# A two-layer block with four attention mixers in float32: three engines get written orders of their own

## What is computed

```python
for l in range(DEPTH):
    x = x + 0.5 * swiglu(rms_norm(x, ffn1_norm[l]), ffn1_w_gate[l], ffn1_w_up[l], ffn1_w_down[l])
    p = rms_norm(x, mix_norm[l]) @ w_in[l]            # 2464 columns, split in four
    a = neighbourhood_mixer(...)                      # group A: local attention with a bias
    b = mla_mixer(...)                                # group B: latent q and kv, up-projections
    c = diff_mixer(...)                               # group C: difference of two softmaxes
    d = gqa_mixer(...)                                # group D: grouped heads, rotated q and k
    x = x + concat(a, b, c, d) @ w_out[l]
    x = x + swiglu(...)                               # FFN2; then a norm
```

## Time and profile before

| What | us |
|---|---|
| Median of 3 runs | 1319.37 |
| Lowest and highest of them | 1311.88, 1321.9 |
| The profiled execution | 1319.89 |
| Its span, first to last instruction | 1317.6 |
| First mixer, about | 196 to 346 |
| Second mixer, about | 710 to 862 |

### The profile page before, as it was taken

The page is one execution under the profiler, slowest core; times in us unless marked ns, Lnnn a source line. Parts: engine busy times, 40 slices in busy tenths (PEclk is TensorE's granted clock), DMA queues, the critical chain, the costliest instruction groups (busy, mean ns, idle before and its releaser), DMA issues.

```text
span 1317.6 us, 24755 instructions
## 1 busy us (share of the span) xinstructions
PE 1265.6 (96%) x10500; PEld 1239.5 (94%) x10500; DVE 841.5 (64%) x1059; ACT 640.0 (49%) x850; POOL 78.7 (6%) x57
## 2 busy tenths in 40 slices
PE   6999999988999999999999997999999999999997
PEld 6999999978999999999999996899999989899995
DVE  5766677775676666876667686476666754446665
ACT  4433346754543334533335764453333554766542
POOL 1110011210000000000000211000000000000000
PEclk9999999986999999999999995799999999999999
DMA  8876665320565655566665530256655655415542
GB/s 287 219 227 206 191 224 172 114 87 2 182 200 193 191 191 192 170 199 195 194 219 163 166 132 12 65 165 219 192 191 191 200 178 174 128 58 168 176 152 105
DMA packets 169514, 220.33 MB, mean 167 GB/s; under 512 B 5280, under 2 KB 152480, under 8 KB 169312
## 3 DMA queue, kind: packets, MB, share of 16 engines
q1 hardware_dynamic: 165680, 213.66, 50.8%
q0 software_dynamic: 2080, 2.48, 1.0%
q10 hardware_dynamic: 1680, 3.13, 0.7%
HBM read 218.15 MB, written 3.42 MB: 168 GB/s over the span
## 4 chain that ended last, share of the span: by engine, by line
PE 86%; ACT 6%; DVE 5%; issue 1%; DMA 1%; SPq 0%; POOLq 0%; POOL 0%; DVEq 0%; ACTq 0%
PE pj L433 12%; PE pj L437 12%; PE pj L436 12%; PE acc L437 8%; PE acc L436 8%; PE acc L433 8%; PE tr L433 6%; PE tr L437 6%; PE tr L436 6%; PE acc L616 4%; ACT probs L994 2%; ACT w_hi L875 1%; PE tr L608 1%; DVE w_lo L1186 1%; PE tr L586 1%
## 5 line engine op out<-in xcount | busy, mean ns | idle before, releaser
L1186 DVE TENSOR_TENSOR w_lo<-raw,w_hi 128x2048 fp32r<-128x2048 f32 (+2 forms) x206 | 459.4, 2230 | 241.7 <-ACT w_hi L875 240.3
L875 ACT ACTIVATE w_hi<-raw 128x2048 fp32r<-128x2048 f32 (+2 forms) x206 | 381.2, 1854 | 395.3 <-PE pj L433 142.0
L433 PE MATMUL pj<-hT_hi,w_hi 128*128 128x256 f32 x992 | 277.2, 279 | 3.0 <-DVE w_lo L1186 2.4
L437 PE MATMUL pj<-hT_hi,w_lo 128*128 128x256 f32 x992 | 275.8, 278 | 0.0
L436 PE MATMUL pj<-hT_lo,w_hi 128*128 128x256 f32 x992 | 275.7, 278 | 0.0
L437 PE MATMUL acc<-act_hi,w_lo 128*128 128x256 f32 x704 | 194.3, 276 | 0.0
L433 PE MATMUL acc<-act_hi,w_hi 128*128 128x256 f32 x704 | 194.3, 276 | 0.0
L436 PE MATMUL acc<-act_lo,w_hi 128*128 128x256 f32 x704 | 194.3, 276 | 0.0
L433 PEld LDWEIGHTS pj<-hT_hi,w_hi 128*128 128x128 f32 x992 | 187.5, 189 | 4.5 <-DVE w_lo L1186 2.6
L436 PEld LDWEIGHTS pj<-hT_lo,w_hi 128*128 128x128 f32 x992 | 187.3, 189 | 0.0
L437 PEld LDWEIGHTS pj<-hT_hi,w_lo 128*128 128x128 f32 x992 | 187.1, 189 | 0.0
(11 more groups left out here) (212 smaller groups left out, 1989.6 us busy)
## 6 DMA issues: line engine op xcount, KB each, us to landing
raw<-in_w_in SPq DMA_DIRECT2D x47, 1024.0 KB, 5.3
raw<-in_ffn_w_up SPq DMA_DIRECT2D x44, 1024.0 KB, 5.3
raw<-in_ffn_w_down SPq DMA_DIRECT2D x44, 1024.0 KB, 5.0
raw<-in_ffn_w_gate SPq DMA_DIRECT2D x43, 1024.0 KB, 5.4
raw<-in_w_out SPq DMA_DIRECT2D x12, 1024.0 KB, 4.9
raw<-in_w_proj_a SPq DMA_DIRECT2D x4, 512.0 KB, 3.5
raw<-in_w_proj_b SPq DMA_DIRECT2D x4, 512.0 KB, 3.9
raw<-in_w_proj_c SPq DMA_DIRECT2D x4, 512.0 KB, 3.4
```

What stands on the lines that cost most here:

```text
L433: ins = pe.matmul(out, lhs[0], rhs[0], start=first, stop=False, **kw)
L437: return pe.matmul(out, lhs[1], rhs[0], start=False, stop=last, **kw)
L875: act.activation(w_hi[r % RING][:, 0:w], raw[r % RING][:, 0:w], ACT.Copy).then_inc(hi_set, 1)
L1186: dve.tensor_tensor(w_lo[r % RING][:, 0:w], raw[r % RING][:, 0:w], w_hi[r % RING][:, 0:w].bitcast(F32), ALU.subtract).then_inc(lo_set, 1)
```

## The change

The one list becomes three: ORDER for TensorE (with the norms at its end, since only their numbering is read from it), ORDER_ACT and ORDER_DVE. Looking ahead by two slots is now a step of its own, ("ahead", step), which stands where it is wanted; VectorE's means of x too. In TensorE's list some steps move:

- slots: proj 3 now comes before 4, 6 before 5, 8 before 7 before 9 (it was 9, 7, 8), and wout C before A, B, D;
- latent between scores 0 and 1;
- pv 2 and turn B before probs 3, pv 3 between scores 4 and 5, probs 5 before probs 4, pv 4, score 6, pv 5, score 7 alternating (it was pv 4, probs 5, pv 5, scores 6, 7);
- yturn A before pv 7, yturn C before pv 8 and 9, yturn D between wout C and A.

In ScalarE's list the roundings stand ahead of evacuations, probs 0 before the evacuation of proj 2, and norm D before the copies of probs 3; after the last units yturn C, a rounding, norm yD, yturn B, yturn D. In VectorE's list means comes before the first rounding, prep D still follows scores 4 and 5 and still stands ahead of pv 4, soft 4 and 5 stand together ahead of pv 4, pv 3 ahead of score 4, and scores 8 and 9 ahead of norm yC and yturn A. No instruction's shape or number changes.

```diff
-ORDER = [("proj", 0), ("proj", 1), ("norm", "A"), ("proj", 4), ("prep", "A"), ("proj", 3), ("norm", "latent"),
-         ("turn", "A"), ("prep", "latent"), ("proj", 5), ("score", 0), ("score", 1), ("latent", 0),
-         ("proj", 6), ("norm", "C"), ("soft", 0), ("soft", 1), ("proj", 2), ("probs", 0), ("latent_up", 0),
-         ("prep", "C"), ("probs", 1), ("pv", 0), ("norm", "B"), ("turn", "C"), ("pv", 1), ("score", 2),
-         ("score", 3), ("soft", 2), ("soft", 3), ("proj", 9), ("prep", "B"), ("proj", 7), ("probs", 2),
-         ("norm", "yA"), ("proj", 8), ("probs", 3), ("pv", 2), ("turn", "B"), ("pv", 3), ("norm", "D"),
-         ("score", 4), ("score", 5), ("prep", "D"), ("soft", 4), ("probs", 4), ("pv", 4), ("soft", 5),
-         ("probs", 5), ("pv", 5), ("score", 6), ("score", 7), ("turn", "D"), ("soft", 6), ("soft", 7),
-         ("probs", 6), ("prep", "yA"), ("norm", "yB"), ("probs", 7), ("pv", 6), ("pv", 7), ("norm", "yC"),
-         ("yturn", "A"), ("score", 8), ("score", 9), ("soft", 8), ("prep", "yB"), ("prep", "yC"),
-         ("soft", 9), ("probs", 8), ("probs", 9), ("pv", 8), ("pv", 9), ("yturn", "B"), ("norm", "yD"),
-         ("prep", "yD"), ("yturn", "C"), ("wout", "A"), ("wout", "B"), ("yturn", "D"), ("wout", "C"),
-         ("wout", "D")]
+ORDER = [("proj", 0), ("proj", 1), ("proj", 3), ("proj", 4), ("turn", "A"), ("proj", 6), ("score", 0),
+         ("latent", 0), ("score", 1), ("proj", 5), ("proj", 2), ("probs", 0), ("latent_up", 0), ("probs", 1),
+         ("pv", 0), ("turn", "C"), ("pv", 1), ("score", 2), ("score", 3), ("proj", 8), ("proj", 7), ("probs", 2),
+         ("proj", 9), ("pv", 2), ("turn", "B"), ("probs", 3), ("score", 4), ("pv", 3), ("score", 5), ("probs", 5),
+         ("probs", 4), ("pv", 4), ("score", 6), ("pv", 5), ("score", 7), ("turn", "D"), ("probs", 6), ("probs", 7),
+         ("pv", 6), ("yturn", "A"), ("pv", 7), ("score", 8), ("score", 9), ("probs", 8), ("probs", 9),
+         ("yturn", "C"), ("pv", 8), ("pv", 9), ("yturn", "B"), ("wout", "C"), ("yturn", "D"), ("wout", "A"),
+         ("wout", "B"), ("wout", "D"), ("norm", "A"), ("norm", "latent"), ("norm", "C"), ("norm", "B"),
+         ("norm", "yA"), ("norm", "D"), ("norm", "yB"), ("norm", "yC"), ("norm", "yD")]
+ORDER_ACT = [("ahead", ("proj", 0)), ("ahead", ("proj", 1)), ("proj", 0), ("ahead", ("proj", 3)), ("proj", 1),
+             ("norm", "A"), ("ahead", ("proj", 4)), ("proj", 3), ("proj", 4), ("norm", "latent"), ("turn", "A"),
+             ("ahead", ("proj", 6)), ("proj", 6), ("score", 0), ("score", 1), ("latent", 0), ("ahead", ("proj", 5)),
+             ("proj", 5), ("norm", "C"), ("ahead", ("proj", 2)), ("probs", 0), ("proj", 2),
+             ("ahead", ("latent_up", 0)), ("latent_up", 0), ("probs", 1), ("norm", "B"), ("turn", "C"),
+             ("score", 2), ("score", 3), ("ahead", ("proj", 8)), ("proj", 8), ("ahead", ("proj", 7)),
+             ("ahead", ("proj", 9)), ("norm", "yA"), ("probs", 2), ("proj", 7), ("proj", 9), ("turn", "B"),
+             ("norm", "D"), ("probs", 3), ("score", 4), ("score", 5), ("probs", 5), ("probs", 4), ("score", 6),
+             ("score", 7), ("turn", "D"), ("probs", 6), ("norm", "yB"), ("probs", 7), ("yturn", "A"),
+             ("norm", "yC"), ("score", 8), ("score", 9), ("probs", 8), ("probs", 9), ("yturn", "C"),
+             ("ahead", ("wout", "C")), ("norm", "yD"), ("yturn", "B"), ("yturn", "D"), ("ahead", ("wout", "A")),
+             ("ahead", ("wout", "B"))]
+ORDER_DVE = [("means", 0), ("ahead", ("proj", 0)), ("ahead", ("proj", 1)), ("norm", "A"), ("ahead", ("proj", 3)),
+             ("prep", "A"), ("norm", "latent"), ("ahead", ("proj", 4)), ("prep", "latent"), ("score", 0),
+             ("score", 1), ("ahead", ("proj", 6)), ("latent", 0), ("soft", 0), ("norm", "C"),
+             ("ahead", ("proj", 5)), ("ahead", ("proj", 2)), ("ahead", ("latent_up", 0)), ("prep", "C"),
+             ("soft", 1), ("pv", 0), ("norm", "B"), ("pv", 1), ("score", 2), ("score", 3), ("soft", 2), ("soft", 3),
+             ("ahead", ("proj", 8)), ("prep", "B"), ("ahead", ("proj", 7)), ("norm", "yA"), ("pv", 2),
+             ("ahead", ("proj", 9)), ("norm", "D"), ("pv", 3), ("score", 4), ("score", 5), ("prep", "D"),
+             ("soft", 4), ("soft", 5), ("pv", 4), ("score", 6), ("pv", 5), ("score", 7), ("soft", 6), ("soft", 7),
+             ("prep", "yA"), ("norm", "yB"), ("pv", 6), ("pv", 7), ("score", 8), ("score", 9), ("norm", "yC"),
+             ("yturn", "A"), ("prep", "yC"), ("prep", "yB"), ("soft", 8), ("soft", 9), ("pv", 8), ("yturn", "C"),
+             ("pv", 9), ("norm", "yD"), ("prep", "yD"), ("yturn", "B"), ("yturn", "D"), ("ahead", ("wout", "C")),
+             ("ahead", ("wout", "A")), ("ahead", ("wout", "B"))]
...
-                for step in ORDER:
+                for step in ORDER_ACT:
                     kind, k = step
+                    if kind == "ahead" and k != MIX_SLOTS[-1]:
+                        look_ahead(SLOT_OF[k], l)
...
-                for step in ORDER:
+                for step in ORDER_DVE:
                     kind, k = step
-                    if kind == "proj":
-                        look_ahead(SLOT_OF[step], l)
-                        if step == ORDER[0]:
-                            means(3 * l + 1)
+                    if kind == "ahead" and k != MIX_SLOTS[-1]:
+                        look_ahead(SLOT_OF[k], l)
+                    elif kind == "means":
+                        means(3 * l + 1)
```

More of the change, by code:

```diff
@@ L282, in build @@
         pj2, tr2, _, _ = number(ORDER2, pj_end, tr_end, pj_fills, tr_fills)
-        PREP_SET = [s[1] for s in ORDER if s[0] == "prep" and s[1][0] != "y"]
-        YNORM_SET = [s[1][1] for s in ORDER if s[0] == "prep" and s[1][0] == "y"]
+        PREP_SET = [s[1] for s in ORDER_DVE if s[0] == "prep" and s[1][0] != "y"]
+        YNORM_SET = [s[1][1] for s in ORDER_DVE if s[0] == "prep" and s[1][0] == "y"]
         U = len(UNITS)
@@ L1059, in _ @@
                     elif kind == "latent_up":
-                        look_ahead(UP_AT, l)
                         for j in range(4):
@@ L1080, in _ @@
                         gain_out_y(l, tr_[step] - g, K_BETA, [g])
-                    elif kind == "wout":
-                        if step != ORDER[-1]:
-                            look_ahead(SLOT_OF[step], l)
                     elif kind == "score":
@@ L1468, in _ @@
                             ins.then_inc(tr_free[f % 2], 1)
-                    elif kind == "latent_up":
-                        look_ahead(UP_AT, l)
                     elif kind == "score":
```

## The result

The changed kernel took 1326.59 us in the median of 20 runs (1322.61 to 1341.28), the kernel before 1321.02 us in 20 runs beside them. The ratio is 1.0081, 95% interval 1.0053 to 1.0110. The profiled execution took 1325.68 us, 5.8 us more than that of before. The forecast was no change, 1319.4 us.

What follows compares the result with a forecast made beforehand. Only the mixers could give: a chain of short links through three engines, with TensorE holes of 10.7 us each and half clock. Per mixer +0.3 and -0.35 made about 0: 1319.4 us, no change, range 1303 to 1328.

Steps and rivals of the forecast that it cites:

- (a): Up to scores 3: low half and norm A's power in time, cost 0; later evacuation of proj 2, +0.45 us.
- (b): Proj 8, 7, 9: roundings and prep B in time, cost 0; score 4 starts at 274.75, +0.3 us.
- (c): Scores 4 and 5 to pv 4: later maximum and four copies in a row make pv 4 2.7 us late.
- (d): Scores 6 to pv 7: the hole of 3.27 us splits, and scores 8 start only 0.85 us late.
- the clock: Score 7 and turn D may run at full clock: -0.35 us a mixer, bounds -3.5 and +1.7.
- (e): Scores 8 to first wout: earlier maximum 8 makes everything up, yturn C's wait delays pv 8; together +0.3 us.
- (f): Wouts: norm yD and the slot of wout B come in time, cost 0; otherwise that slot's 2.3 us.
- Rival 3: Scores 4 to 7: the delay of (c) is not made up, 3.35 us a mixer, 1326.1 us; chance 0.12.
- The other signs: Mixers: qkT wait below 1.5 us, probsT wait 2 or more each mixer, first wout within 1 us.

Runs made afterwards that it cites:

- E2: Changed kernel with a one-column memset on VectorE between the mean and the next subtraction, at four places; ratio to the kernel before 1.0056, median 1326.45 us.
- e5: Changed kernel with one-column memsets on VectorE between mean and subtraction, VectorE also waiting for its own means first; ratio to the kernel before 0.9997.
- E6: Changed kernel with the steps and slots up to score 3 in the old order, the rest new; ratio to the kernel before 0.9994.
- e1: Changed kernel with VectorE waiting for GpSimd's power after the means of x and of norms A, latent and C; ratio 1.0113, median 1333.93 us.
- e3: Changed kernel with yturn A moved back ahead of scores 8 and 9 in VectorE's list; ratio to the kernel before 1.0088.
- e4: Changed kernel with pv 3 and units 4 and 5 back in the old order in all three lists; ratio to the kernel before 1.0072.
- f1: Old order up to turn B, then units one at a time through ScalarE and VectorE, prep D cut in two; 0.9943 of the kernel before, repeat 0.9928.

## Why the prediction was wrong

**The step that failed is (a), up to scores 3.** It says of means and the low half "That fits with 0.2 us to spare. Cost 0", and of norm A's power and prep A that they "are ready at 217.3". The low half did come in time; no product waited for a w_lo inside a mixer. But means ahead of the subtraction puts the power for xr beside that subtraction, and it took 2.70 us instead of 0.72. Norm A's power came to stand 0.04 us behind a subtraction instead of ahead of it: it ended at 220.03, and prep A 1.2 us later. That cost 0.97 + 0.89 us of holes and made turn A 2.2 us late, where the sum had 0. E2, with xr's power alone still blocked, is 1.3 us late there, and e5, with neither, 0.1. The other term of (a), +0.45 for the evacuation of proj 2, was right in size: from probs 0 to probs 1 it took 6.2 us in the changed kernel and in e5, 5.7 before. With the collisions away, e5 reaches score 4 0.2 and 0.4 us late, where (b) had +0.3.

I took GpSimd's durations as fixed. They were the one term whose neighbour changed.

**(c) was right in kind, too small in size.** Pv 4 was to come 10.25 us after score 4, where it was 7.8. It came 11.6 and 11.3 after. The copies of probs 5 and 4 took 3.66 us (284.92 to 288.58), not 2.4, because the transposes between them (12 in 2.86 us) came in the way; the hole went where it was put (1.85 + 0.78).

**(d) made up nothing, and missed the clock.** Pv 4 was to be 2.7 us late and score 8 only 0.85, since that stretch was to shrink to 20.2 us (285.0 to 305.2). It took 22.8 in both mixers, before 22.1 and 23.8. Less the 2.5 and 2.6 us of the early part, pv 4 came 3.8 and 3.6 us late and score 8 4.5 and 2.5. The changed kernel ran this stretch at half clock throughout; the window that stood at 0.78 in the earlier trace rows reads

```profile
295.00:300.00 5.00, 4.41 (x22) 4.09 (x22) 1.98 (x9) 2.07 (x8) 0.00 (x0) 0.50 0.00 0
```

with TensorE busy 4.41 of 5 us instead of 1.90. Scores 6 and 7 show the price, before

```profile
290.24 2.74 PE L596 MATMUL acc<-qkT 32*128 32x256 f32 x16
```

and changed

```profile
293.04 2.08 PE L620 MATMUL acc<-qkT 32*128 32x256 f32 x8 [0.68 <-DVE hn L1544]
...
299.32 2.08 PE L620 MATMUL acc<-qkT 32*128 32x256 f32 x8 [0.59 <-DVE hn L1544]
```

1.4 us more for the two. I had taken -0.35 for the clock, with +1.7 and -3.5 as the bounds. Up to score 8 it cost these 1.4 us, and in the first mixer 1.7 more in pv 4 (3.65 us, before 1.97). Behind score 8 the clock came back: pv 8 and 9 took 3.7 us in the first mixer and 4.1 in the second instead of 6.9, and the wouts 1.9 and 1.7 less. Over the whole late part that is an estimated 2 to 3 us a mixer in favour of the change. By the rule on transposes that the prediction quotes from the Trainium skill's page TensorE: Matmul & The Clock Gate (Part 4: PE-mode transpose), the value was +1.7. Its sign fits the stretch up to score 8 and not the mixer as a whole, and no run separates the transposes from the rest.

**(e): the arrival of maximum 8.** It was to come 1.0 us after score 8's start instead of 2.1. It came 2.17 us after it, as before (2.11). Scores 8 and 9 are 3.95 us of TensorE at half clock (the row at 311.50), so maximum 8 had its score only then; norm yC and yturn A had filled a time in which it could not start. Moved behind maximum 9, yturn A's low half held the bank that the second half of probs 8 wants: the hole of 2.88. (e) moved the step and priced what waited for yturn C, but not who waits for yturn A's bank.

**The balance of the late part.** From score 4 to the first wout it lost 2.5 and 0.6 us, and the wouts took 22.4 us instead of 24.2 and 24.0, at full clock from the start. Together about 0, the forecast sum, but by luck: the delays of (c) to (e) were larger than forecast, and a clock that I had not forecast covered them. E6 bears the sum out in time: 0.9994. (f) held: no slot came late.

**The rivals.** Rival 3 had its size right by luck, 1326.1 us, and its place wrong: the delay that lasted came from (a)'s collisions, not from (c). The other signs: the wait of turned q and k, 6.4 us in the earlier trace rows, fell to 4.1 in 4, not below 1.5; that of turned probabilities fell from 6.1 to 1.6, against my "2 us or more each mixer", since the exponentials now are named ahead of them:

```profile
PE tr L632 <- DVE hT_lo L1411: 5.5, 2, 2.9
PE tr L632 <- ACT probs L1018: 4.7, 6, 1.8
PE tr L632 <- ACT qkT L968: 4.1, 4, 1.8
...
PE acc L640 <- ACT probsT L1028: 1.6, 2, 0.8
```

The clock stayed at 0.969 (0.968 before), and the first wout came 5.0 and 3.2 us later, not within 1.

## What to carry to other kernels

When a step is moved, look on GpSimd's timeline for what runs beside it on VectorE, before and after, and compare starts to the hundredth: a GpSimd instruction that was first by 0.04 us can be second after any reordering, and then costs the whole length of VectorE's, here up to 2.3 us. If it carries a small value that others wait for, put one short instruction between its trigger and the next long two-input operation, and look whether GpSimd now starts first; at the means that took a wait of VectorE for its own result as well (e5). Waiting for GpSimd's result gained nothing here (e1). Where three engines pass short pieces along, let one unit go through alone rather than two in step, and cut long work that stands ahead of a release.

## What was not expected of the hardware

- A GpSimd power of 2 elements took 0.72 us or 2.70 to 2.85, and one of 16 took 2.90 or 5.00, by whether VectorE's subtraction had started 0.03 to 0.16 us ahead. A copy of 128x256 took 0.39 (before, e2, e5), and 2.02 with a subtraction that had started 0.5 us ahead. The maximum that starts at 276.39 reads the accumulator alone; it started 0.04 us ahead of a power of 12 elements, and that took 2.27 us, no more than in the changed kernel with nothing beside its start.
- VectorE hardly pays behind a power: 2.32 us with the power first, 2.29 otherwise. Behind GpSimd's operation on 128x1536 it pays the rest of that operation's length: 4.12 us.
- A hole filled need not shorten the chain, since the clock behind it can fall at another place (e3, e4). In one kernel run twice, f1 and its repeat, the first wout started at 117.3, 124.0, 123.2 and 119.5 us of the four mixers, with the same order of work: the granted clock fell at another place each time. In the window 285 to 290 it was 0.99 in one run and 0.50 in the other. That may be where the spread between executions comes from; what decides the place was not tried.
